# Exchanging the rotary halves of q and k: eight ScalarE copies per head replaced by eight small transfers within SBUF

## What is computed

```python
u = x * (1 + scale) + shift                       # (shift, scale, gate) = c @ W_mod + b_mod
q, k, v, z_a, B, C, xc, z_b, g_a, g_b = split(u @ w_in)
# rotary on each 64-wide half head:
t1, t2 = split(t, 2, axis=-1)
t = concatenate([t1 * cos - t2 * sin, t2 * cos + t1 * sin], axis=-1)
# 8 heads of differential attention:
o = (softmax(q1 k1^T) - lambda * softmax(q2 k2^T)) @ v
y_a = rms_norm(o) * (1 - lambda_init) * silu(z_a)
y_b = B * causal_conv3(C * xc) * silu(z_b)
h = sigmoid(g_a) * (y_a @ P_a) + sigmoid(g_b) * (y_b @ P_b)
out = LayerNorm(alpha * x + gate * (h @ w_out))
```

## Time and profile before

| | us |
|---|---|
| runs (3) | 1499.01, 1501.14, 1500.59; median 1500.59 |
| the profiled execution, its own time | 1499.35 |
| its span, first to last instruction | 1497.7 |
| TensorE busy | 1474.7 |
| VectorE busy | 875.5 |
| ScalarE busy | 518.8 |
| GpSimd busy | 48.3 |

### The profile page before, as it was taken

The page is one execution under the profiler, slowest core; times in us unless marked ns, Lnnn a source line. Parts: engine busy times, 40 slices in busy tenths (PEclk is TensorE's granted clock), DMA queues, the critical chain, the costliest instruction groups (busy, mean ns, idle before and its releaser), DMA issues.

```text
span 1497.7 us, 18490 instructions
## 1 busy us (share of the span) xinstructions
PE 1474.7 (98%) x6640; PEld 1212.6 (81%) x6640; DVE 875.5 (58%) x1206; ACT 518.8 (35%) x740; POOL 48.3 (3%) x91
## 2 busy tenths in 40 slices
PE   6999999999999999999999999999999999999996
PEld 5888888888888888888888888888888888888885
DVE  7987877567575675756757568333432323444447
ACT  2334654253442534425344253232122121421120
POOL 0000000000000000000000000100000000000000
PEclk9999999999999999999999999999999999999998
DMA  9999533543544435444254442542223322363222
GB/s 358 392 325 323 189 115 118 149 124 93 157 121 143 130 92 153 127 133 140 85 155 132 133 141 78 199 146 85 84 93 103 99 97 86 110 253 112 84 84 112
DMA packets 211974, 219.18 MB, mean 146 GB/s; under 512 B 8417, under 2 KB 160353, under 8 KB 211169
## 3 DMA queue, kind: packets, MB, share of 16 engines
q1 hardware_dynamic: 200736, 176.72, 36.2%
q0 software_dynamic: 10096, 35.66, 7.8%
q10 hardware_dynamic: 1106, 6.32, 1.1%
HBM read 211.33 MB, written 7.34 MB: 146 GB/s over the span
## 4 chain that ended last, share of the span: by engine, by line
PE 90%; DVE 6%; DMA 1%; issue 1%; SPq 1%; ACT 0%; DVEq 0%; ACTq 0%
PE acc L1351 28%; PE acc L1353 28%; PE acc L1352 28%; DVE mod_sum L851 3%; DMA raw<-in_w_in 1%; PE sc L1486 1%; PE misc L1509 1%; DVE w_lo L824 1%; PE sc L1500 1%; SPq L396 0%; DVE act_lo L898 0%; PE misc L1492 0%; DVE mod_sum L848 0%; DVE act_lo L925 0%; ACT w_hi L532 0%
## 5 line engine op out<-in xcount | busy, mean ns | idle before, releaser
L1351 PE MATMUL acc<-act_hi,w_hi 128*128 128x512 f32 x1472 | 577.8, 393 | 2.3 <-DVE act_lo L898 2.3
L1353 PE MATMUL acc<-act_hi,w_lo 128*128 128x512 f32 x1472 | 573.9, 390 | 0.0
L1352 PE MATMUL acc<-act_lo,w_hi 128*128 128x512 f32 x1472 | 573.7, 390 | 0.0
L532 ACT ACTIVATE w_hi<-raw 128x1024 fp32r<-128x1024 f32 (+2 forms) x258 | 267.7, 1045 | 734.3 <-PE acc L1353 576.3
L824 DVE TENSOR_TENSOR w_lo<-raw,w_hi 128x1024 fp32r<-128x1024 f32 x254 | 306.5, 1215 | 368.2 <-ACT w_hi L532 367.7
L1351 PEld LDWEIGHTS acc<-act_hi,w_hi 128*128 128x128 f32 x1472 | 276.9, 188 | 61.6 <-DVE act_lo L898 3.1
L1353 PEld LDWEIGHTS acc<-act_hi,w_lo 128*128 128x128 f32 x1472 | 276.7, 188 | 58.1
L1352 PEld LDWEIGHTS acc<-act_lo,w_hi 128*128 128x128 f32 x1472 | 276.9, 188 | 56.9 <-issue 0.2
L1080 DVE SCALAR_TENSOR_TENSOR bias_acc<-bias_w,mod,bias_acc 128x512 f32<-128x512 f32 x48 | 36.1, 751 | 122.8 <-DMA bias_w<-in_w_in 122.8
L1351 PE MATMUL acc<-y_hi,w_hi 128*128 128x512 f32 x256 | 99.7, 389 | 0.0
L1353 PE MATMUL acc<-y_hi,w_lo 128*128 128x512 f32 x256 | 99.6, 389 | 0.0
(11 more groups left out here) (196 smaller groups left out, 1126.6 us busy)
## 6 DMA issues: line engine op xcount, KB each, us to landing
raw<-in_w_in SPq DMA_DIRECT2D x258, 256.0 KB, 6.2
raw<-in_w_tail SPq DMA_DIRECT2D x32, 1024.0 KB
raw<-in_w_in SPq DMA_DIRECT2D x25, 1024.0 KB
w_mod_in<-in_w_mod SPq DMA_DIRECT2D x32, 512.0 KB, 8.6
w_mod_in<-in_w_mod SPq DMA_DIRECT2D x16, 1024.0 KB, 7.6
gate_in<-in_w_mod POOLq DMA_DIRECT2D x32, 512.0 KB, 4.2
bias_w<-in_w_in POOLq DMA_DIRECT2D x48, 256.0 KB, 3.2
res<-in_x ACTq DMA_DIRECT2D x1, 4096.0 KB, 14.8
```

The costliest lines, as they stand in the source:

```text
L532: return act.activation(dst, src, ACT.Copy)
L1351: pe.matmul(dst, a_hi, b_hi, start=first, stop=False)
L1352: pe.matmul(dst, a_hi, b_lo, start=False, stop=False)
L1353: return pe.matmul(dst, a_lo, b_hi, start=False, stop=last)
```

## The change

In `drain_head`, right behind the drain of q's bank, ScalarE waits for its own copy and issues four DMAs from `q_raw` to `q_rot`, 32 partitions by 2 KB each; the same behind k's. The eight copies and their place behind `z_a` are gone. Each of q and k gets a semaphore of its own, which VectorE awaits at 64 per head.

```diff
-        qk_swapped = sem("qk_swapped")
+        swapped = [sem("q_swapped"), sem("k_swapped")]
...
                     copy(plain[:, :], acc[:, n, :]).then_inc(bank_drained[n], 1)
+                    act.wait_ge(bank_drained[n], i * 2 + (1 + FIRST_BLOCKS + BASE))
+                    for g in range(4):
+                        to = g ^ 1
+                        act.dma_start(turned[32 * to:32 * to + 32, :], plain[32 * g:32 * g + 32, :]
+                                      ).then_inc(swapped[n], 16)
                 act.wait_ge(bank_full[2], i * 2 + (1 + FIRST_BLOCKS))
                 act.wait_ge(v_turned, i + BASE)
                 copy(v_f[:, :], acc[:, 2, :]).then_inc(bank_drained[2], 1)
                 act.wait_ge(half_done, z_done)
                 copy(z_a[:, :], acc[:, 3, :]).then_inc(bank_drained[3], 1)
-                for n, (plain, turned) in enumerate(((q_raw, q_rot), (k_raw, k_rot))):
-                    act.wait_ge(bank_drained[n], i * 2 + (1 + FIRST_BLOCKS + BASE))
-                    for g in range(4):
-                        to = g ^ 1
-                        ins = copy(turned[32 * to:32 * to + 32, :], plain[32 * g:32 * g + 32, :])
-                    ins.then_inc(qk_swapped, 1)
...
-                    dve.wait_ge(qk_swapped, i * 2 + n + 1)
+                    dve.wait_ge(swapped[n], i * 64 + 64)
```

## The result

The changed kernel takes 1506.77 us (median of 6 runs, 1505.7 to 1509.29) against 1500.37 of the kernel before in the runs beside it: a ratio of 1.0045, interval 1.0035 to 1.0055, slower by 6.4 us. The forecast of no change was wrong, and the time lies 1.2 us above the range.

The account below looks back on a forecast made before the run. TensorE, busy throughout the head passes, was taken as the bound: 0.22 us in the first drain and 0 elsewhere made 1499.6 us for a profiled execution, 1500.8 us as median, range 1499.0 to 1505.6 us.

Parts of the forecast that it names:

- The forecast of no change: Whole kernel: no change that counts, stalls from 0 to 0.37 us per head, 1500.8 us; chance 0.69.
- the copies are worth 0: ScalarE in the heads: removing eight copies, 5.1 us per head, gains nothing, as they lie beside TensorE's matmuls.
- The place that decides: Start of each convolution block: TensorE's wait for bank 2, expected free at 302.39 and wanted at 302.56.
- X: ScalarE's queue: time from one DMA issue to the next, taken as 0.47 us, bounds 0.36 and 0.56.
- the issues hold up the drain of v: Rival at TensorE's wait for bank 2: longer issues make it late, 4.2 us, 1504.8 us at 0.55 per issue; chance 0.22.
- The sum up to the weight load: Second drain: issues, waits and copies from q's copy end at 296.94 free bank 2 at 298.63 + 8X.
- my 302.56: Bank 2 of the next block: the time TensorE loads its weights, taken as when the bank is wanted.
- The first drain: Bank 2 at the first drain: q's copy ends late at 203.40, so bank 2 is late by 0.22 us.
- The landing: Exchange transfers within SBUF: 3.2 us taken from bias_w, bounds 2.7 and 6.8 us; k landed at 304.3.
- the limit of 6.45: Chain to the scores: k's landing may take 6.45 us before TensorE feels it.
- The rival of late landing: TensorE's wait for qk_split behind half 1: transfers landing 1.46 us apart cost 21 us, 1522 us; chance 0.06.
- The dispatch of about 50 ns: ScalarE's queue: the skill's figure would make eight issues 0.4 us; the forecast followed the trace's 0.42 to 0.52 each.

Follow-up runs that it names:

- no_exchange: Kernel before with each four exchange copies replaced by one whole 128-partition copy, leaving out the exchange of halves; 1500.78 us, ratio 1.0005.
- k_behind_z: Changed kernel with k's wait and four issues moved behind z_a's copy, so four issues stand ahead of v's; 1500.08 us, ratio 0.9997.
- probe: Kernel before plus 16 issues on ScalarE's queue ahead of the last stage: four from HBM, twelve within SBUF of three shapes; 1528.05 us in one run.
- all_behind_z: Changed kernel with all eight issues of q and k moved behind z_a's copy; 1500.89 us, ratio 1.0003.
- both_at_once: Against the changed kernel, q and k share one tensor, moved by four 128 KB transfers behind k's copy; 1503.08 us, ratio 1.0014.

## Why the prediction was wrong

*That TensorE bounds the heads and the copies are worth 0:* right. no_exchange and the passes of k_behind_z show it.

*The place that decides:* right. I had named TensorE's wait for bank 2 behind v_f's copy, with eight issues ahead of it, and a break-even of 0.49 us for X; the rival "the issues hold up the drain of v" (0.22) is what happened.

*X, the time from issue to issue: this is the term that failed.* I took 0.47 us from c_col and b_col, "plain static copies on the same queue, as these are", and bounded it by 0.56. It is 2.46 / 4 = 0.62. The rows were of the same queue and of plain shape, but every one has HBM at one end; the probe shows 0.44 for that kind and 0.61 within SBUF. I had noticed that no row shows a transfer within SBUF for the landing, and bounded that one widely; for the issue I let the queue's rows stand as bounds. The sum up to the weight load held: from the end of q's copy to that load I had 5.45 us (3.76 for the issues, 1.20 for the copies, 0.49 of hand-overs), and the second drain has 306.13 - 299.63 = 6.50 (4.92, 1.20, 0.38).

*What a late load costs* I had slightly wrong, and it hardly shows in the total. The third drain, which is like the five behind it:

```profile
393.76 0.60 ACT L532 ACTIVATE q_raw<-acc 128x512 f32<-128x512 f32 x1 [0.38 <-PE acc L1352]
...
400.88 0.19 PEld L1350 LDWEIGHTS acc<-act_hi,w_hi 128*128 128x128 f32 x1 [0.94 <-ACT v_f L532]
400.88 0.50 PE L1350 MATMUL acc<-act_hi,w_hi 128*128 128x512 f32 x1 [0.52 <-ACT v_f L532]
```

From the end of q's copy at 394.36 to the load are 6.52 us, so the load is 6.52 - 5.45 - 0.17 = 0.90 late by my sum. But my 302.56 was the load's time, and its matmul came 0.23 later, at 302.79. Now the matmul starts with the load: it is only 0.68 late (400.88 instead of 400.20), and the next one adds 0.11. That is 0.79, which is 0.11 less than the load is late; the five drains behind it have 0.74 to 0.80. In the second drain, whose q copy is late, it is 0.88 and 0.11. Together these make 5.7 of the 6.0 us that the seven passes are longer (0.86 each).

*The first drain* is later than the others, as said, for q's late copy: bank 2's first matmul is 1.1 us late where the later ones have 0.7. The prediction puts it 0.39 behind the others (0.94 against 0.55 at X = 0.56), which held; its 0.22 was all that is left of this at X = 0.47. It did not have the second drain, which is late as well (its q copy stands behind a w_hi that waited for its weights).

*The landing:* 3.2 us taken, 3.2 measured for k, 3.6 for q; the limit of 6.45 was never reached in the changed kernel. The rival of late landing was wrong for it, and so was its mechanism, transfers that land 1.46 us apart: all_behind_z lands most of k's in 2.0 us each, issued 0.64 apart. But the wait that it names is real, and both_at_once ran into it.

*The dispatch of about 50 ns* (the Trainium skill, page "DMA: Bandwidth & Descriptors", section "Anatomy of one DMA") would have made the change free. The issue measured here is twelve times that. The section's table is of the path that starts at GpSimd; for ScalarE's and SyncE's queues the rows here decide.

*The range* reached to X = 0.56. With 0.62 the sum gives 298.63 + 8 x 0.62 = 303.59, 1.03 us late in seven drains and 1.42 in the first: 8.6 us, 1509, against the 7.2 us that the head stage of the profile lost. Of the difference about 0.1 us per drain are hand-overs that I had too long, and another 0.1 is the cost of a late load, as above. So with X right the sum would have been 1.4 us above what the head stage lost; the error that mattered is X.

## What to carry to other kernels

A DMA issue is an instruction of its engine's order, and what stands behind it waits: count the issues ahead of every copy that frees a PSUM bank, at the price of that kind of transfer, here 0.6 us within SBUF. Where the engine has slack, put them behind the last such copy, or on a queue with nothing urgent behind it; with the eight small transfers both gave the time of the kernel before, and neither was faster. What waits for the landing then has less to spare, as the one wait of all_behind_z shows. And a bound needs a row of the same kind, source and destination included; where there is none, the range has to reach past the rows that there are.

## What the hardware showed that I had not expected

- The issue of a transfer within SBUF takes 0.61 us on ScalarE's queue and 0.59 on SyncE's; from HBM it takes 0.44 (probe) and 0.37. Rows (32 or 128) and bytes (2, 64 or 128 KB) change it by 0.01 us at most. The first of a set is often shorter on ScalarE's queue, at 0.51 to 0.53.
- Within SBUF, 64 KB land 2.0 us after the issue in seven of the eight heads of all_behind_z, where the last weight loads were issued about 4 us earlier, and up to 5.2 us after it for q in the changed kernel, issued beside such loads.
- ScalarE issues DMAs while copies that it has already handed on are running (300.24 against 300.55 in k_behind_z).
- In the profile of all_behind_z the granted clock is 0.946 over the whole span, yet the seven passes took 659.2 us, 1.7 more than before (0.9 of it the one wait for k_lo), and the run 1500.89: the shown clock did not cost what its number suggests. What the other 0.8 us are was not found.
